# Router matmuls on the plain residual rows, modulation folded into the router's weights, rows turned inside the last projection

## The reference

```python
x  = x + gate1 * (merged @ w_out[l])
h2 = rms_norm(x, norm2_g[l]) * (1.0 + scale2) + shift2
# in hier_moe, with xf = h2:
p_g      = softmax(xf @ w_rg + b_rg)          # 4 group logits
e_logits = xf @ w_re + b_re                   # 32 expert logits
# best group, two best experts in it, then for each slot of each expert:
y = (silu(xi @ w1[e]) * (xi @ w3[e])) @ w2[e] * weight
x = x + gate2 * y
```

## Time and profile before

| | us |
|---|---|
| median of 3 runs | 1614.45 |
| lowest, highest | 1613.6, 1615.25 |
| the profiled execution | 1613.26 |
| its span, first to last instruction | 1611.5 |
| PE busy | 1511.1 (94%) |
| DVE, ACT, POOL busy | 524.5, 356.1, 106.8 |
| mean granted TensorE clock | 0.97 |

### The profile page before, as it was taken

The page is one execution under the profiler, slowest core; times in us unless marked ns, Lnnn a source line. Parts: engine busy times, 40 slices in busy tenths (PEclk is TensorE's granted clock), DMA queues, the critical chain, the costliest instruction groups (busy, mean ns, idle before and its releaser), DMA issues.

```text
span 1611.5 us, 20221 instructions
## 1 busy us (share of the span) xinstructions
PE 1511.1 (94%) x7966; PEld 679.3 (42%) x7966; DVE 524.5 (33%) x1085; ACT 356.1 (22%) x689; POOL 106.8 (7%) x140
## 2 busy tenths in 40 slices
PE   3999999999999999999999999869999899989897
PEld 3444445454545455444444455433333233323232
DVE  6576223223233224722223255562111111111111
ACT  4312322223233712111111133311111011101010
POOL 1000000000000000000000000100111111111101
PEclk9999899999999999999999999869999999999999
DMA  9760001010101011011130562367999999999992
GB/s 368 269 261 23 30 0 53 1 52 0 31 8 27 13 27 27 23 43 39 39 112 5 228 254 91 131 236 284 414 412 403 415 409 404 409 416 401 418 374 72
DMA packets 67564, 290.94 MB, mean 181 GB/s; under 512 B 11124, under 2 KB 35743, under 8 KB 52127
## 3 DMA queue, kind: packets, MB, share of 16 engines
q1 hardware_dynamic: 60912, 273.08, 42.7%
q0 software_dynamic: 6576, 16.79, 4.2%
HBM read 276.21 MB, written 19.92 MB: 184 GB/s over the span
## 4 chain that ended last, share of the span: by engine, by line
PE 50%; DMA 8%; DVE 2%; issue 0%; ACT 0%; SPq 0%; POOL 0%; POOLq 0%; DVEq 0%
PE PS L661 47%; DMA WK<-in_expert_w 5%; DMA R<-in_expert_w 3%; PE PS L1048 1%; PE PS L1070 1%; PE PS L988 0%; DVE R L1434 0%; DVE R L1426 0%; ACT R L1144 0%; DVE R L1431 0%; DVE R L1430 0%; PE PS L919 0%; DVE WK L1431 0%; POOL out_rows L625 0%; DVE R L1799 0%
## 5 line engine op out<-in xcount | busy, mean ns | idle before, releaser
L661 PE MATMUL PS<-R 128*32 128x512 f32 (+5 forms) x4051 | 747.1, 579 | 35.0 <-ACT R L1144 8.9
L661 PEld LDWEIGHTS PS<-R 128*32 128x32 f32 (+4 forms) x4051 | 262.9, 129 | 408.0 <-issue 382.3
L661 PE MATMUL PS<-R,HT 128*128 128x512 f32 (+1 forms) x768 | 342.8, 602 | 3.7 <-DVE HT L1431 3.0
L661 PE MATMUL PS<-HT,R 128*32 128x512 f32 (+2 forms) x1184 | 316.4, 603 | 3.5 <-DMA WK<-in_expert_w 1.8
L1426 DVE TENSOR_TENSOR R<-R,PS 128x512 f32<-128x512 f32 (+1 forms) x95 | 71.6, 772 | 470.4 <-PE PS L661 470.3
L661 PEld LDWEIGHTS PS<-R,HT 128*128 128x128 f32 x768 | 145.2, 193 | 175.1 <-issue 173.7
L661 PEld LDWEIGHTS PS<-HT,R 128*32 128x32 f32 (+1 forms) x1184 | 106.1, 134 | 146.2 <-issue 144.2
L1144 ACT ACTIVATE R<-PS 128x512 f32<-128x512 f32 (+4 forms) x128 | 76.6, 608 | 397.4 <-PE PS L661 256.8
L661 PE MATMUL PS<-WK,R 128*32 128x512 f32 (+1 forms) x384 | 94.9, 617 | 4.3 <-DMA R<-in_expert_w 4.3
L1144 ACT ACTIVATE R<-PS,S,A 128x128 f32<-128x128 f32 x88 | 33.2, 457 | 193.3 <-PE PS L1048 193.3
L625 POOL DMA_INDIRECT out_rows<-R x37 | 53.6, 1448 | 307.4 <-DVE R L1434 171.6
(11 more groups left out here) (236 smaller groups left out, 847.0 us busy)
## 6 DMA issues: line engine op xcount, KB each, us to landing
R<-in_expert_w SPq DMA_DIRECT2D x67, 2048.0 KB, 34.9
HT<-in_expert_w SPq DMA_DIRECT2D x20, 2048.0 KB, 32.0
R<-in_ada_w SPq DMA_DIRECT2D x24, 1024.0 KB, 7.4
WK<-in_expert_w SPq DMA_DIRECT2D x9, 2048.0 KB, 35.2
R<-in_w_in SPq DMA_DIRECT2D x6, 2048.0 KB, 8.0
R<-in_w_in SPq DMA_DIRECT2D x16, 512.0 KB, 4.6
R<-in_x SPq DMA_DIRECT2D x2, 2048.0 KB, 13.6
R<-in_x SPq DMA_DIRECT2D x8, 512.0 KB, 4.1
```

What stands on the lines that cost most here:

```text
L661: return nc.tensor.matmul(o, l, r, start=a, stop=z)
```

## The change

The router reads the turned rows of x itself. A tile's transposes read `xh[u]` instead of `xn[u]` (`turn_x1`, one half of the features at a time), as soon as `residual` has written that half, and the copies out of PSUM are plain: one instruction on ACT for bank 4 (`x1_turned`), one on DVE for bank 5 (`turned`). The reciprocal root multiplies the logits in `choose`, in the instruction that adds the bias. The normalised rows are still written to `xn_rows`, for the experts. The weights `wr` are multiplied by A2 once, before attention; S2 times `wr` is summed over the features by eight matmul calls against a matrix of ones, and DVE adds that row to the router's bias. Since the plain rows are turned in their natural order of features and the weights were loaded in the permuted one, `wr` is written to memory and read back in the other order by two DMAs of SP.

The order changes too. On PE, `turn_x1(t - 1)` with both halves stands between the two halves of `out_proj(t)`, and `route(t - 1)` after the first two of the second half's eight calls; in the last tile each half's transposes stand inside or behind the projection. On DVE, `choose(t - 1)` stands between the two halves of `residual(t)`. SP reloads `xh[u]` after the transposes of the tile in it instead of after its squares. POOL fills constants for the tables after it has staged the last tile instead of after the last projection.

The core of the diff:

```diff
 # SP
+            load_section(2, O_DV)
+            load_section(3, O_GQK)
+            e.wait_ge(s["small_ld"], 16 * N_SMALL)
+            e.wait_ge(s["mods_col"], 2)
+            e.dma_start(wr_rows.rearrange("(p k) n -> p k n", p=P), wr[:, :, :]).then_inc(s["small_ld"], 16)
+            e.wait_ge(s["small_ld"], 16 * (N_SMALL + 1))
+            e.dma_start(wr[:, :, :], wr_rows.rearrange("(k p) n -> p k n", p=P), ...)
+            load_section(4, O_GR)
+            load_section(5, O_GV)
...
                     store_x(2 * i + u, u)
                     e.wait_ge(x1_st[u], 16 * (i + 1))
-                    e.wait_ge(s["x1_sq"], 2 * (2 * i + u) + 2)
+                    e.wait_ge(s["h2_tr"], 2 * (2 * i + u) + 2)
                     e.dma_start(xh[u], x_v[2 * i + u + 2]).then_inc(xh_ld[u], 16)
 # POOL
-            e.wait_ge(s["mo_mm"], 2 * NT)
+            e.wait_ge(s["ms_ready"], NT - 1)
             e.memset(onesb, 1.0)
 # PE, before attention
             e.wait_ge(s["glr_done"], 2)
-            attend(0, lambda i: section_tile(2, i), 4 + 2 * NT + 1)
+            e.wait_ge(s["kT_done"], NT)
+            e.wait_ge(s["mods_col"], 2)
+            for k in range(KT):
+                last = mm(bank(7)[:, 0:NR], onesf[:, :], wr_shift[:, k, :], k == 0, k == KT - 1)
+            last.then_inc(s["mods_ps"], 1)
...
+            attend(0, values_tile, 4 + 2 * NT + 1)
 # PE, the stage
+            def turn_x1(t, u, half):
+                e.wait_ge(s["x1_ready"], 2 * t + half + 1)
+                e.wait_ge(s["h2_evd" if half else "h2_eva"], t + 1)
...
+            def step(t, u):
+                out_proj(t, u, 0)
+                turn_x1(t - 1, 1 - u, 0)
+                turn_x1(t - 1, 1 - u, 1)
+                out_proj(t, u, 1, 0, 2)
+                route(t - 1, 1 - u)
...
+                    step(2 * i + 2 - u, u)
+                    out_proj(2 * i + 2 - u, u, 1, 2, KT)
+            step(NT - 1, 1)
+            out_proj(NT - 1, 1, 1, 2, 6)
+            turn_x1(NT - 1, 1, 0)
+            out_proj(NT - 1, 1, 1, 6, KT)
+            turn_x1(NT - 1, 1, 1)
             route(NT - 1, 1)
 # ACT
+            def x1_turned(t, u):
+                e.wait_ge(s["rt_mm"], t + 1)
+                e.wait_ge(s["h2_tr"], 2 * t + 1)
+                act(h2T[u][:, 0:4, :].rearrange(...), bank(4), ACT.Copy).then_inc(s["h2_eva"], 1)
...
+            x1_turned(NT - 2, 0)
+            x1_square(NT - 1, 1, 0)
+            x1_turned(NT - 1, 1)
+            x1_square(NT - 1, 1, 1)
+            x1_norm(NT - 1, 1)
 # DVE, before attention
+            tt(wr_shift, wr[:, :, :], spread(S2 ...), ALU.mult).then_inc(s["wr_read"], 1)
+            tt(wr[:, :, :], wr[:, :, :], spread(A2 ...), ALU.mult).then_inc(s["mods_col"], 1)
...
+            e.wait_ge(s["mods_ps"], 2)
+            tt(rbias[:, :], rbias[:, :], bank(7)[:, 0:NR], ALU.add).then_inc(s["mods_col"], 1)
 # DVE, the stage
+            def turned(t):
+                e.wait_ge(s["rt_mm"], t + 1)
+                e.wait_ge(s["h2_tr"], 2 * t + 2)
+                v.tensor_copy(h2T[t % 2][:, 4:8, :].rearrange(...), bank(5)).then_inc(s["h2_evd"], 1)
...
-                tt(logits[:, t, :], bank(6)[:, 0:NR], rbias[:, :], ALU.add).then_inc(s["rt_done"], 1)
+                stt(logits[:, t, :], bank(6)[:, 0:NR], stat[:, 2, t % 2:t % 2 + 1], rbias[:, :], ALU.mult, ALU.add)
...
+            for t in range(NT):
+                residual(t, 0)
+                if t >= 1:
+                    turned(t - 1)
+                    choose(t - 1)
+                residual(t, 1)
+                mean_square(t)
+                if t == NT - 1:
+                    turned(t)
+                normalised(t)
             choose(NT - 1)
```

More of the change, by code:

```diff
@@ L385, in _, with load_section @@
                     load_ada(g, j, True)
-            for n, off in ((2, O_DV), (3, O_GQK), (4, O_GR), (5, O_GV)):
+            def load_section(n, off):
                 e.wait_ge(s["w_ld"], 16 * n)
@@ new lines, in x1_square, with x1_norm @@
+            def x1_square(t, u, half):
+                c = slice(half * 512, (half + 1) * 512)
+                e.wait_ge(s["x1_ready"], 2 * t + half + 1)
+                act(xn[u][:, c], xh[u][:, c], ACT.Square, accum_out=stat[:, 2 * half, u:u + 1]).then_inc(s["x1_sq"], 1)
+            def x1_norm(t, u):
+                e.wait_ge(s["x1_sq"], 2 * t + 2)
+                e.wait_ge(s["x1_rs"], 2 * t + 1)
+                act(stat[:, 3, u:u + 1], stat[:, 2, u:u + 1], ACT.Sqrt, scale=1.0 / D, bias=stat[:, 1, u:u + 1]).then_inc(s["x1_sd"], 1)
+                e.wait_ge(s["x1_rs"], 2 * t + 2)
+                act(xn[u][:, 512:D].rearrange("p (k q) -> p q k", k=4), xh[u].rearrange("p (q k) -> p q k", k=KT)[:, :, 4:KT],
+                    ACT.Copy, scale=stat[:, 2, u:u + 1]).then_inc(s["xn2_ready"], 1)
@@ new lines, in x1_turned @@
+            def x1_turned(t, u):
+                e.wait_ge(s["rt_mm"], t + 1)
+                e.wait_ge(s["h2_tr"], 2 * t + 1)
+                act(h2T[u][:, 0:4, :].rearrange("p k q -> p (k q)"), bank(4), ACT.Copy).then_inc(s["h2_eva"], 1)
+            for half in range(2):
+                x1_square(0, 0, half)
+            x1_norm(0, 0)
+            with e.Fori(0, NT // 2 - 1) as i:
+                for u in (1, 0):
+                    t = 2 * i + 2 - u
+                    x1_turned(t - 1, 1 - u)
+                    for half in range(2):
+                        x1_square(t, u, half)
+                    x1_norm(t, u)
@@ L1823, in residual @@
                     stat[:, 2, u:u + 1], ALU.mult).then_inc(s["xn2_ready"], 1)
-            def modulate2(t):
-                u = t % 2
-                e.wait_ge(s["h2_tr"], t + 3)
-                for k in range(4):
-                    last = tsc(h2T[u][:, k, :], bank(4)[:, k * P:(k + 1) * P],
-                               A2[:, k:k + 1], ALU.mult, S2[:, k:k + 1], ALU.add)
-                last.then_inc(s["h2_evd"], 1)
             def choose(t):
@@ L1836, in choose @@
                 c = slice(t, t + 1)
-                tt(logits[:, t, :], bank(6)[:, 0:NR], rbias[:, :], ALU.add).then_inc(s["rt_done"], 1)
+                stt(logits[:, t, :], bank(6)[:, 0:NR], stat[:, 2, t % 2:t % 2 + 1], rbias[:, :], ALU.mult, ALU.add).then_inc(s["rt_done"], 1)
                 e.wait_ge(s["rt_done"], t + 2)
@@ L1851, in choose @@
                 rt(tsc(oh2[:, t, :], iota_m[:, :], sel_id, ALU.is_equal))
-            residual(0)
-            modulate2(0)
-            for t in range(1, NT):
-                residual(t)
-                if t == 1:
-                    rt(v.memset(prior_b[:, 0, :], 0.0))
-                choose(t - 1)
-                modulate2(t)
+            for t in range(NT):
+                residual(t, 0)
+                if t >= 1:
+                    turned(t - 1)
+                    if t == 1:
+                        rt(v.memset(prior_b[:, 0, :], 0.0))
+                    choose(t - 1)
[4 more added lines that the diff above has]
+                normalised(t)
             choose(NT - 1)
```

100 lines of the change are left out of this document (44 added, 56 removed).

## The result

The changed kernel took 1616.55 us (median of 20 runs, 1611.94 to 1625.39), the kernel before 1613.34 (20 runs, 1611.46 to 1615.25). The medians differ by 3.2 us; the ratio is 1.0026, 95% interval 1.0013 to 1.0038, or 2.1 to 6.1 us slower. So the changed kernel is slower, by little. 1615.0 had been forecast.

The account below looks back on a forecast made before the run. PE was taken to bound the kernel (half of the span), then DMA. Terms 1.7 + 1.8 - 2.9 = +0.6 us on the profiled 1613.26, on the median 1615.0 us; range 1610.5 to 1618.5 us.

Parts of the forecast that it names:

- 1.7 us for the calls before attention: Before the first scores on PE: eight added calls (16 instructions) are all path, +1.7 us; bounds 0 to 3.6.
- rival 2: Before attention: added matmuls fill PE's pause, the half-clock stretch goes, cost 1.7 and gain 1.7, 1613.3 us; 17% alone.
- 1.8 us for the third tile: Stage's third tile: PE waits 1.8 us for DVE's copy, behind the add awaiting a late x; bounds 0 to 3.6.
- nothing in the change moves that load: Third tile: the late load of x stays where it was, so DVE's add starts at 949.37 as before.
- 2.9 us for the tail: Stage's end: logits 6.5 us earlier, but the gather meets full DMA engines, so 2.9 us gained; bounds 1.8 to 7.7.
- the 3.6 that the prediction had said would be taken back: First gather: amid weight loads it takes 11.2 us instead of 5.0, so the tail's 6.5 us shrinks to 2.9.
- rival 1: First gather after the stage: not held up, tail gives 6.5 us, 1611.4 us (7.7 and 1610.2 at full clock); 16% alone.
- Rival 4: Stage's loop: DVE's copy is late in every tile, 0.5 us in each of six steps, +3.6, 1618.0 us; 7%.
- Rival 3: Third tile: a pause past 2.3 us throttles PE, next stretch costs 2.7 us more, +3.9, 1618.3 us; 10%.

Follow-up runs that it names:

- b2: Kernel before plus eight products of 36 columns that nobody reads, placed ahead of the first scores: 1616.72 us, ratio 1.0019.
- g1_none: Changed kernel with the first gather before the weight loads, third tile's copy ahead of its add, the eight calls and the shift left out: 1604.95 us, ratio 0.9947.
- e2: Changed kernel with DVE's copy of bank 5 put ahead of the add that waits for x, in the third tile alone: 1613.18 us, ratio 1.0002.
- f2: Changed kernel with three of SP's five weight preloads issued behind the first two tiles' stores and loads of x: 1613.04 us, ratio 1.0001.
- e1: Changed kernel with SP waiting for the first gather to land before it issues four weight loads: 1612.37 us, ratio 1.0006.
- b1: Kernel before plus eight products of 36 columns that nobody reads, in PE's wait between first and second scores: 1613.62 us, ratio 1.0003.
- f1: Changed kernel without the eight S2 calls, the wait for them and the add to the bias: 1610.03 us, ratio 0.998.

## Why the prediction was right or wrong

The time was inside the range and 1.5 us above the forecast. Part of that nearness is luck: the forecast stood on a median of 1614.45 from three runs, where 20 runs give 1613.34, and the change itself was forecast at +0.6 us and measured at +3.2 (+2.2 in the repeat). All three terms were found where the prediction had put them, but none had its size: 1.7, 1.8 and -2.9 us were forecast, the two traces have 2.95, 0.65 and -3.7. In the traces the errors largely cancel (sum -0.1); in the medians they do not, and the excess over the forecast is the first term's and the second's.

**1.7 us for the calls before attention: mis-sized.** The calls' own time was right (1.88). What failed is the sentence "all path: +1.7 us", which gave the calls no effect on the clock, and rival 2, by which the slow stretch might go, failed too: it doubled, from 3.4 to 6.8 us. In the profiled pair the term is 2.95 us, alone in the kernel before it is 3.0 by the medians (b2), and in the changed kernel 4.8 to 6.2. The rest of it is half clock, near 196 us and, in three of eight profiles, also at 520 to 660 us. The calls come ahead of the pause and do not shorten it; with calls inside it the clock stayed at 1.00 there, in all three profiles, but so it did in g1_none with nothing in it, so that the filling keeps the clock up is not shown. What is shown is that calls ahead of the pause cost more than their own 1.9 us: the eight profiles with them are at least 2.9 us longer from bracket to stage than the six others. Why PE's clock later in attention depends on what it did at 190 us is open. It was not tried to move the calls further ahead, into the low-rank work.

**1.8 us for the third tile: right in place, in its cause and in that no other tile has one, too large in the trace and too small in the median.** The profiled pauses are 0.6 to 1.2 us. The prediction took over the time at which DVE's add had started, 20.0 us behind the stage's first transposes; "nothing in the change moves that load" failed, since in the five profiles with the pause it started at 19.2 to 19.8 us. The first output store, which gates the load of x, took 19.4 to 20.0 us in them. The medians of e2 and f2 say 3 us. A half clock behind the pause, seen in one profile of five, explains part of this; the whole is not accounted for.

**2.9 us for the tail: the mechanism right, the size 0.8 too small in the trace.** The logits came 6.6 us earlier against the stage's start, 7.2 without the pause (5.5 to 7.7 forecast). The gather took 10.98 us against 11.2, was issued amid the weight loads, and PE waited for a DMA. Without the pause (e2) stage to expert rows is 134.11 us, 3.7 less than before. With the gather ahead of the loads it is 130.4, another 3.7: the 3.6 that the prediction had said would be taken back (6.5 less 2.9). So rival 1 was wrong, and its price about right: without the delay the tail gives 7.4 us, between its 6.5 and 7.7. The medians put the tail's gain as the change has it at 3.2 to 6.4 us: e2 is 0.2 us below before, to which the calls' price, 3.0 to 6.2, is added. Why that is more than the trace's 3.7 isn't located.

Why the gather takes 11 us can be read from the packets. Alone, in e1 from 1058.2 to 1062.4 us, it has (all packets, then those of its queue):

```profile
DMA packets 144, 0.31 MB, mean 73 GB/s; under 512 B 69, under 2 KB 69, under 8 KB 144
q0 software_dynamic: 144, 0.31, 24.7%
```

That is 75 packets of 4 KB and 69 tiny ones: 75 rows, 0.31 MB, not the 128 rows and half a megabyte of the prediction. Over the whole run this queue moves 16.79 MB, which is the 2048 filled slots (two for each of the 1024 tokens) gathered and written back once, so empty slots move no row. After the change, from 1058.4 to 1065.1 us (packets, MB, share):

```profile
q1 hardware_dynamic: 170, 2.52, 88.0%
q0 software_dynamic: 166, 0.39, 14.7%
```

The loads and the gathers (the next one is queued behind the first) moved one packet each in turn, 170 and 166, but one seventh of the bytes went to the gathers. 144 packets of the first gather with as many of 14.8 KB (2.52 MB / 170) between them are 2.4 MB, 5.6 us at the 435 GB/s of this stretch (an estimate); from 1058.4 to the landing at 1065.06 it is 6.7. The other part of the delay lies ahead of the first packet, which moved 4.4 us after the issue here and 1.9 in e1; why is not shown. The Trainium skill (DMA: Bandwidth & Descriptors, Queues, rings and completion order) says that an engine alternates between its queues packet by packet; the trace agrees, 170 to 166. The prediction had read that rule as equal bytes, and had added the whole time of half a megabyte at half the rate, 2.4 us, to the 5.0 of rows 9, where only the excess over full rate belonged.

**Rival 4** (a late copy in every tile) did not happen: one bracket in the stage's loop. **Rival 3** happened in one of five profiles, at 1.04 us; its rule, that the length of the pause decides, does not hold: 1.09 and 1.19 us left the clock up, and the kernel before already had half clock behind 1.56 us and none behind 1.8 us.

## What to carry to other kernels

Small work that must go somewhere on the busiest engine can cost more than its own time when it stands ahead of a wait, and next to nothing inside the wait: here 3 to 6 us against 0.1 for 1.9 us of products, at one place of one kernel. When a chain of dependent work is shortened, look at what the last link competes with: a small indirect load issued onto DMA engines full of large packets gave back half of the gain (3.7 of 7.4 us), and one wait in the issuing queue restored it. Where the clock varies, one profile can miss half of a cost that medians show, and can show a gain (b1) that whole runs do not have.

## What the runs showed of the hardware that was not expected

- With the same instructions up to there, PE reached 190.8 us in some executions and 192.9 in others; the difference arises at half clock between 30 and 57 us.
- Half clock in attention (186 to 930 us) took 13.7, 20.5, 23.9 or 37.5 us in the 14 profiles, and the length of attention followed: 733.1 to 733.5, 736.6 to 736.7, 739.6 to 739.8, 746.4 us.
- A pause of 1.04 us was once followed by 3.4 us at half clock, and four pauses of 0.6 to 1.2 us were not.
- The stretch behind the 1.56 us wait near 195 us was 3.4 us at half clock in before and f1, 6.8 in all eight profiles with calls ahead of the scores, and absent in the three with the calls inside the wait. It was also absent in g1_none, where the wait is empty (PE's window behind it, same columns):

```profile
194.00:198.00 4.00, 4.00 (x13) 1.00 0.00 0
```

- A gather of 75 rows of 4 KB took 4.1 us on idle DMA engines and 11.0 beside weight loads that fill them; 2.5 us of the difference passed before its first packet.
